# RWKV mixer: the first pair's preparation moved in among the feature projections

## The chip, the cores and the metric

The kernel runs on one core of one Trainium2 chip. A NeuronCore has a matrix engine (TensorE, PE), whose weight loads are shown apart as PEld, a vector engine (VectorE, DVE), an activation engine (ScalarE, ACT), GpSimd (POOL) and SyncE (SP), which here issues DMAs. The engines run their own instruction streams and wait for each other on semaphores. TensorE's clock is at 1.2 or 2.4 GHz; the profile gives it as the granted clock, 0.50 or 1.00. The metric is the device time of one execution in microseconds; smaller is better. The kernel before takes 3924.44 us (median of 3 runs, 3923.59 to 3925.01).

## The reference

One inference step of a two-layer decoder for 1024 prompt tokens and 8 x 8 sample tokens (1088 in all). Layer 0 has sparse attention (NSA) and RWKV-7 time mixing side by side, layer 1 gated linear attention (GLA); each is followed by a SwiGLU feed-forward. The change touches the RWKV-7 part only. Cut to what matters:

```
p  = rmsnorm(x) @ w_in                      # columns: r, k, v (512 each), xw 64, xa 64, xg 128
ps = p + mu * (p_prev - p)                  # token shift
z  = w0 + tanh(xw) @ wB;  w = exp(-exp(-softplus(-z) - 0.5))      # decay
a  = sigmoid(a0 + xa @ aB)
g  = sigmoid(xg) @ gB
kk = heads(k * k_k);  kk = kk * rsqrt(max(sum(kk * kk), 1e-24))
k  = heads(k * (1 + (a - 1) * k_a))
# per token and head: S = S*w + (S @ -kk)(kk*a)^T + v k^T;  y = S @ r
y  = groupnorm(y) * ln_w + ln_b + sum(r * k * r_k) * v           # the last term is the bonus
return y * g
```

## The kernel before

Activations lie transposed: 128 features on the partitions, 1088 tokens along the free axis, cut into chunks of 384, 384 and 320 (`CH`), so that one product of a 128-column weight tile is 8 x 3 matmuls into three PSUM banks. The 8 heads are worked as 4 pairs (128 columns). PSUM has 8 banks; the part at hand uses them as two groups of three, banks 0 to 2 and 3 to 5.

The program is a row of blocks. Each block is one function's instruction streams for all engines, and a barrier of all engines stands between two blocks. Around the change the row is: load inputs; `rmsnorm`; `rwkv_features`; `rwkv_prepare`; `rwkv_heads`; then `nsa_project` and the rest.

- `rwkv_features` projects five tiles in the order 0 to 4: tile 0 is xw and xa ("lora" below), tile 1 xg ("gate"), tiles 2, 3, 4 r, k, v of the first pair ("receptance", "keys", "values"). PE (L1422) fills one group of banks while ACT (L1435) copies the other to `raw`, and DVE (L1454, L1393 to L1397, L1457) mixes each token with the one before it. ACT then takes tanh (L1441) and sigmoid (L1443) of the two lora tiles. SP loads the weight tile after next as soon as a product is done (L1412).
- `rwkv_prepare` makes what the first pair's scan needs. PE: z (L1473), a (L1475), the sum of squares of kk over each head (L1480), the sum of the bonus (L1484). ACT: two sigmoids (L1491, L1494), a square root (L1497), three exponentials of the summed decay (L1499, L1501, L1503). DVE: everything between, with a reciprocal (L1527) and a scan (L1515), up to L1546.
- `rwkv_heads` scans the first pair while it projects and prepares the next ones; its first PE instruction is L1643 (scores of the first group of four 64-token chunks). The pieces beside its scan are set by a table written out by hand (`beside`), which the change does not touch.

The order on each engine is the order in which the code is written; no scheduler moves anything. A wait (`next`) is put on the engine's next instruction.

Of the kernel before, what the change touches and what calls it, by code (L numbers as in the profile page):

```python
# [17 lines left out]
ALU = mybir.AluOpType  # L18
# [4 lines left out]
P = 128  # L23
D = 1024
KT = D // P
NP = 1024
# [1313 lines left out]
def rwkv_mix(g, d, late):  # L1340
    nc = g.nc
    with ExitStack() as ctx:
# [29 lines left out]
        s = signals(nc, ctx, "rw_", "product raw_ready mixed_in za_ready kk_squared kk_summed kk_root "  # L1372
# [7 lines left out]
        rwkv_features(g, d, b, s, w_here, small)  # L1380
        rwkv_prepare(g, d, b, s, st_here)
# [18 lines left out]
def rwkv_features(g, d, b, s, w_here, small):  # L1400
    nc = g.nc
    tiles = range(5)
    with nc.Block() as block:
        @block.sync
        def _(sp):
            for i in range(2):
                sp.dma_start(b.w[i][:, :, :], d.w_rwkv[i]).then_inc(w_here[i], 16)
            sp.dma_start(b.lw[:, :, :].rearrange("p a n -> p (a n)"), d.lora).then_inc(small, 16)
            sp.dma_start(b.shift[:, :, :], d.shift).then_inc(small, 16)
            for i in tiles:  # L1410
                s.product.next(sp)
                sp.dma_start(b.w[i % 2][:, :, :], d.w_rwkv[RWKV_USES[i + 2]]).then_inc(w_here[i % 2], 16)  # L1412

        @block.tensor
        def _(pe):
            for x, i in enumerate(tiles):
                pe.wait_ge(w_here[i % 2], 16 * (i // 2 + 1))
                if x >= 2:
                    s.raw_ready.next(pe)
                for k in range(KT):  # L1420
                    for c, (o, n) in enumerate(CH):
                        mm = pe.matmul(g.ps[:, 3 * (x % 2) + c, 0:n], b.w[i % 2][:, k, :], g.act[:, k, o:o + n], start=(k == 0), stop=(k == KT - 1))  # L1422
                s.product.mark(mm)
            s.raw_ready.next(pe, 2)

        @block.scalar
        def _(act):
            seen = 0
            for x, i in enumerate(tiles):
                s.product.next(act)  # L1430
                if x >= 2 and seen < x - 1:
                    s.mixed_in.next(act, x - 1 - seen)
                    seen = x - 1
                for c, (o, n) in enumerate(CH):
                    a = act.activation(b.raw[x % 2][:, o:o + n], g.ps[:, 3 * (x % 2) + c, 0:n], ACT.Copy)  # L1435
                s.raw_ready.mark(a)
                if i < 2:
                    s.mixed_in.next(act)
                    seen = x + 1
                    if i == 0:  # L1440
                        act.activation(b.lora[0:64, 0, :], b.lora[0:64, 0, :], ACT.Tanh)  # L1441
                    else:
                        act.activation(b.lora[:, 1, :], b.lora[:, 1, :], ACT.Sigmoid)  # L1443
            s.mixed_in.next(act, len(tiles) - seen)

        @block.vector
        def _(dve):
            for n, i in enumerate(tiles):
                out = b.lora[:, i, :] if i < 2 else (b.r[:, :], b.k[:, :], b.v[0])[i - 2]
                x = b.raw[n % 2]  # L1450
                s.raw_ready.next(dve)
                if i == 0:
                    dve.wait_ge(small, 32)
                dve.tensor_tensor(out[:, 1:NP], x[:, 0:NP - 1], x[:, 1:NP], ALU.subtract)  # L1454
                rwkv_mixed(dve, g, b, i, x, out)
                dve.drain()
                s.mixed_in.mark(dve.scalar_tensor_tensor(out, out, g.col["mu"][:, i:i + 1], x, ALU.mult, ALU.add))  # L1457


def rwkv_prepare(g, d, b, s, st_here):  # L1460
    nc = g.nc
    col = lambda name: g.col[name][:, 0:1]
    ps3 = lambda first: [(g.ps[:, first + c, 0:n], o, n) for c, (o, n) in enumerate(CH)]
    bonus_in = b.raw[1]
    with nc.Block() as block:
        @block.sync
        def _(sp):
            sp.dma_start(b.st8[:, :, :], d.srwkv[0]).then_inc(st_here, 16)

        @block.tensor  # L1470
        def _(pe):
            for p, o, n in ps3(0):
                pe.matmul(p, b.lw[0:64, 0, 0:P], b.lora[0:64, 0, o:o + n], start=True, stop=True)  # L1473
            for p, o, n in ps3(3):
                mm = pe.matmul(p, b.lw[64:P, 0, 0:P], b.lora[64:P, 0, o:o + n], start=True, stop=True)  # L1475
            s.za_ready.mark(mm)
            s.kk_squared.next(pe)
            s.a_ready.next(pe)
            for p, o, n in ps3(0):
                mm = pe.matmul(p, g.blk, b.e[:, o:o + n], start=True, stop=True)  # L1480
            s.kk_summed.mark(mm)
            s.bonus_in.next(pe)
            for p, o, n in ps3(3):
# [4 lines left out]
        def _(act):  # L1488
            s.za_ready.next(act)
# [3 lines left out]
            for p, o, n in ps3(3):  # L1493
                a = act.activation(b.a[:, o:o + n], p, ACT.Sigmoid, bias=col("a0"))  # L1494
            s.a_ready.mark(a)
            s.kk_root.next(act)
            s.sq_ready.mark(act.activation(b.e[:, :], b.e[:, :], ACT.Sqrt))  # L1497
            s.decay_read.next(act)
            s.decay.mark(act.activation(b.e[:, :], b.e[:, :], ACT.Exp))  # L1499
            s.decay_read.next(act)  # L1500
            s.decay.mark(act.activation(b.e[:, :], b.cum[:, :], ACT.Exp, scale=-1.0))  # L1501
            s.decay_read.next(act)
            s.decay.mark(act.activation(b.e[:, :], b.cum[:, :], ACT.Exp))  # L1503

# [1298 lines left out]
```

## Time and profile before

| what | value |
|---|---|
| median of 3 runs | 3924.44 us |
| profiled execution | 3919.16 us, span 3917.5 us |
| mean granted clock | 0.950 |
| PE, DVE, ACT, POOL busy | 90%, 37%, 21%, 14% |
| first matmul of `rwkv_features` | 53.27 us |
| first matmul of `rwkv_prepare` | 133.32 us |
| first matmul of `rwkv_heads` | 169.56 us |

Times within the span count from its start. A busy share is an average over stages that differ, so it does not tell what bounds the stage at hand; for that the timeline is read, where each row has the start, the duration, the engine, the line and, in brackets, how long the engine stood idle before and who released it. A product of fp32 operands shows as two records for each matmul.

### The profile page before, as it was taken

How to read it: one execution, taken by the hardware profiler on the slowest of the kernel's cores; microseconds unless marked ns; L12 is line 12 of the kernel's file. 1: busy time of each engine (PE TensorE's matmuls, PEld its weight loads, DVE VectorE, ACT ScalarE, POOL GpSimd, SP SyncE). 2: the span in 40 equal slices, each digit the busy share in tenths (PEclk: the TensorE clock that was granted, in tenths of full speed). 3: DMA queues.
4: the chain of work that ended last, by engine and by line, in shares of the span. 5: the costliest groups of instructions: out<-in, count | busy, mean ns of one | idle time of the engine just before them, and what ended most of it. 6: DMA issues, size and time to landing. Idle time of an engine off the chain costs nothing. (4 is left out here: it accounts for less than half of the span.)

```text
span 3917.5 us, 60103 instructions
## 1 busy us (share of the span) xinstructions
PE 3528.8 (90%) x24871; PEld 2937.1 (75%) x24871; DVE 1444.3 (37%) x2676; ACT 830.0 (21%) x1575; POOL 535.8 (14%) x362
## 2 busy tenths in 40 slices
PE   6698988798877857999999998999997999999996
PEld 3466666654545636999999997666656999999996
DVE  2445645532256654332222333223323332322331
ACT  1132221111045622211111111222212211111110
POOL 0000000001400002422222221000001422222221
PEclk9899999898879978999999999999998999999998
DMA  2000000012310022111111111211122111111112
GB/s 92 20 12 13 24 12 13 30 63 68 88 49 1 2 100 73 50 51 35 52 38 43 48 32 45 85 39 40 65 91 107 50 51 35 52 33 44 52 32 99
DMA packets 77161, 189.07 MB, mean 48 GB/s; under 512 B 30996, under 2 KB 45268, under 8 KB 73956
## 3 DMA queue, kind: packets, MB, share of 16 engines
q1 hardware_dynamic: 64164, 157.97, 12.1%
q0 software_dynamic: 8448, 27.27, 2.2%
q8 instruction: 142, 2.33, 0.2%
q10 hardware_dynamic: 4352, 1.05, 0.2%
q14 instruction: 55, 0.45, 0.0%
HBM read 161.34 MB, written 29.04 MB: 49 GB/s over the span
## 5 line engine op out<-in xcount | busy, mean ns | idle before, releaser
L224 PE MATMUL ps<-ff_x,ff_wh 128*128 128x384 f32 (+1 forms) x3960 | 774.9, 328 | 0.0
L224 PEld LDWEIGHTS ps<-ff_x,ff_wh 128*128 128x128 f32 x3960 | 668.7, 188 | 0.8
L224 PE MATMUL ps<-ff_x,ff_wl 128*128 128x384 f32 (+1 forms) x2112 | 465.5, 328 | 0.0
L224 PEld LDWEIGHTS ps<-ff_x,ff_wl 128*128 128x128 f32 x2112 | 360.8, 188 | 0.0
L531 DVE TENSOR_TENSOR resid<-resid,ps 128x384 f32 (+1 forms) x240 | 113.2, 527 | 383.7 <-PE ps L224 383.7
L2377 PE MATMUL ps<-act,gl_w 128*128 128x384 f32 (+1 forms) x768 | 243.5, 473 | 0.0
L224 PE MATMUL ps<-ff_hh,ff_dh 128*128 128x384 f32 (+1 forms) x1056 | 233.2, 328 | 4.6 <-DVE ff_hl L523 4.6
L224 PE MATMUL ps<-ff_hh,ff_dl 128*128 128x384 f32 (+1 forms) x1056 | 232.7, 328 | 0.0
L224 PE MATMUL ps<-ff_hl,ff_dh 128*128 128x384 f32 (+1 forms) x1056 | 232.7, 328 | 0.0
L2377 PEld LDWEIGHTS ps<-act,gl_w 128*128 128x128 f32 x768 | 144.2, 191 | 89.1 <-issue 9.3
L518 DVE TENSOR_TENSOR ff_prod<-ff_silu,ps 128x384 f32<-128x384 f32 x132 | 62.3, 527 | 349.6 <-PE ps L224 349.6
L224 PEld LDWEIGHTS ps<-ff_hh,ff_dh 128*128 128x128 f32 x1056 | 180.2, 188 | 5.8 <-DVE ff_hl L523 5.8
L224 PEld LDWEIGHTS ps<-ff_hl,ff_dh 128*128 128x128 f32 x1056 | 180.4, 188 | 0.0
L224 PEld LDWEIGHTS ps<-ff_hh,ff_dl 128*128 128x128 f32 x1056 | 180.3, 188 | 0.0
L290 POOL TENSOR_TENSOR ff_wl<-ff_w,ff_wh 128x1024 fp32r<-128x1024 f32 x44 | 111.9, 2542 | 500.3 <-ACT ff_wh L415 500.3
L1676 PE MATMUL ps<-rw_up,rw_low 64*64 64x128 f32 (+1 forms) x1632 | 135.0, 264 | 45.8 <-DVE rw_tri L2059 29.0
L511 DVE TENSOR_TENSOR ff_silu<-ff_stats,ps 128x384 f32<-128x384 f32 x132 | 62.3, 527 | 302.7 <-PE ps L224 302.2
L298 POOL TENSOR_TENSOR ff_dl<-ff_wd,ff_dh 128x512 fp32r<-128x512 f32 (+1 forms) x80 | 111.9, 1404 | 410.7 <-ACT ff_dh L423 410.7
L607 PE MATMUL ps<-np_w,act 128*128 128x512 f32 (+5 forms) x432 | 159.6, 529 | 1.5 <-DVE resid L682 0.9
L1749 PE MATMUL ps<-act,rw_w 128*128 128x384 f32 (+1 forms) x432 | 160.9, 505 | 0.0
L439 ACT ACTIVATE ff_silu<-ff_silu 128x1088 f32<-128x1088 f32 x44 | 49.1, 1115 | 512.7 <-DVE ff_silu L511 512.7
L423 ACT ACTIVATE ff_dh<-ff_wd 128x512 fp32r<-128x512 f32 (+1 forms) x80 | 53.0, 674 | 480.8 <-PE ps L224 426.0
(567 smaller groups left out, 5499.1 us busy)
## 6 DMA issues: line engine op xcount, KB each, us to landing
ff_w<-in_wg SPq DMA_DIRECT2D x44, 512.0 KB, 3.5
ff_w<-in_wu SPq DMA_DIRECT2D x44, 512.0 KB, 3.5
ff_wd<-in_wd POOLq DMA_DIRECT2D x48, 256.0 KB, 3.0
ff_wd<-in_wd POOLq DMA_DIRECT2D x32, 320.0 KB, 3.3
ns_past<-in_cache_slc SPq DMA_DIRECT2D x64, 128.0 KB, 2.1
rw_w<-in_w_rwkv SPq DMA_DIRECT2D x14, 512.0 KB, 3.6
np_w<-in_w_nsa SPq DMA_DIRECT2D x8, 652.0 KB, 8.1
resid<-in_x SPq DMA_DIRECT2D x1, 4352.0 KB
```

What stands on the lines that cost most here:

```text
L224: mm = pe.matmul(g.ps[:, bank + c, 0:n], w[:, k, :], x[:, o:o + n], start=(first and i == 0), stop=(last and i == 2))
L290: pool.tensor_tensor(wl[0][:, :, :], w[0][:, :, :], wh[0][:, :, :].bitcast(F32), ALU.subtract).then_inc(s.gate_lo, 1)
L298: pool.tensor_tensor(dl[t][:, 0:nf, :], wd[t][:, 0:nf, :], dh[t][:, 0:nf, :].bitcast(F32), ALU.subtract).then_inc(s.down_lo, 1)
L423: act.activation(dh[t][:, 0:nf, :], wd[t][:, 0:nf, :], ACT.Copy).then_inc(s.down_hi, 1)
L439: act.activation(silu[:, :], silu[:, :], ACT.Silu).then_inc(s.silu_done, 1)
L511: m = dve.tensor_tensor(silu[:, o:o + n], rs[:, o:o + n], g.ps[:, c, 0:n], ALU.mult)
L518: m = dve.tensor_tensor(prod[:, o:o + n], silu[:, o:o + n], g.ps[:, 3 + c, 0:n], ALU.mult)
L531: m = dve.tensor_tensor(r, r, g.ps[:, 3 * t + c, 0:n], ALU.add)
L607: mm = pe.matmul(g.ps[0:R, b + j, 0:n], x, w[:, k, o:o + n], start=(k == 0), stop=(k == KT - 1))
L1676: mm = pe.matmul(g.ps[h, 5, P * c + 64 * x0:P * c + 64 * x1], low, up, start=True, stop=True)
L1749: mm = pe.matmul(g.ps[:, bank(j, name), 0:m], b.w[n % 2][:, k, :], g.act[:, k, o:o + m], start=(k == 0), stop=(k == KT - 1))
L2377: mm = pe.matmul(out[:, 0:n], w[:, k, :], g.act[:, k, o:o + n], start=(k == 0), stop=(k == KT - 1))
```

## The change

`rwkv_prepare` is gone as a block. Its instructions stand inside `rwkv_features`, whose order of projections is now `RWKV_FIRST` = 0, 3, 2, 1, 4: lora, keys, receptance, gate, values. The two groups of three PSUM banks are used in turn by nine users: lora (banks 0 to 2), keys (3 to 5), receptance (0 to 2), length (3 to 5), z (0 to 2), a (3 to 5), gate (0 to 2), values (3 to 5), bonus (0 to 2). The temporaries that shared buffers with `raw` now use `bt[1]` and `kt[1]`, which the second pair needs only later. The state's load (`st8`) is issued behind the last weight load. Core of the diff:

```diff
-        rwkv_features(g, d, b, s, w_here, small)
-        rwkv_prepare(g, d, b, s, st_here)
+        rwkv_features(g, d, b, s, w_here, small, st_here)
...
+RWKV_FIRST = [0, 3, 2, 1, 4]
...
+    scratch, bonus_in = b.bt[1], b.kt[1]
...
+            project(LORA, 0)
+            project(KEYS, 1)
+            s.raw_ready.next(pe)
+            project(RECEPTANCE, 0)
+            s.raw_ready.next(pe)
+            s.kk_squared.next(pe)
+            for p, o, n in ps3(1):
+                mm = pe.matmul(p, g.blk, b.e[:, o:o + n], start=True, stop=True)
+            s.kk_summed.mark(mm)
+            s.raw_ready.next(pe)
+            pe.wait_ge(small, 32)
+            s.lora_ready.next(pe)
+            for p, o, n in ps3(0):
+                mm = pe.matmul(p, b.lw[0:64, 0, 0:P], b.lora[0:64, 0, o:o + n], start=True, stop=True)
+            s.z_ready.mark(mm)
+            s.kk_root.next(pe)
+            for p, o, n in ps3(1):
+                mm = pe.matmul(p, b.lw[64:P, 0, 0:P], b.lora[64:P, 0, o:o + n], start=True, stop=True)
+            s.za_ready.mark(mm)
+            s.log_ready.next(pe)
+            project(GATE, 0)
+            s.a_ready.next(pe)
+            project(VALUES, 1)
+            s.raw_ready.next(pe)
+            s.bonus_in.next(pe)
+            for p, o, n in ps3(0):
+                mm = pe.matmul(p, g.blk, bonus_in[:, o:o + n], start=True, stop=True)
+            s.bonus_sum.mark(mm)
```

On PE, before, the end of the last projection and the block behind it (L1422 projection, L1473 z, L1475 a, L1480 length, L1484 bonus; "waits" names the semaphores):

```order
93 L1422 MATMUL ps<-act,rw_w 128x320
94 L1403 UNCONDITIONAL_BRANCH [waits rw_raw_ready]
95 L1470 UNCONDITIONAL_BRANCH [waits barrier_Pool_Activation_PE_DVE_SP_release]
96 L1473 MATMUL ps<-rw_lora,rw_lw 128x384 x2
97 L1473 MATMUL ps<-rw_lora,rw_lw 128x320
98 L1475 MATMUL ps<-rw_lora,rw_lw 128x384 x2
99 L1475 MATMUL ps<-rw_lora,rw_lw 128x320
100 L1480 MATMUL ps<-rw_e,const 128x384 [waits rw_a_ready,rw_kk_squared]
103 L1484 MATMUL ps<-resid,const 128x384 [waits rw_bonus_in]
107 L1630 UNCONDITIONAL_BRANCH [waits barrier_Pool_Activation_PE_DVE_SP_release]
```

On PE, changed, the place between the third and the fourth projection, and the end (L1429 projection, L1439 length, L1445 z, L1449 a, L1458 bonus):

```order
59 L1429 MATMUL ps<-act,rw_w 128x320
60 L1439 MATMUL ps<-rw_e,const 128x384 [waits rw_kk_squared,rw_raw_ready]
63 L1445 MATMUL ps<-rw_lora,rw_lw 128x384 [waits rw_lora_ready,rw_small,rw_raw_ready]
66 L1449 MATMUL ps<-rw_lora,rw_lw 128x384 [waits rw_kk_root]
69 L1429 MATMUL ps<-act,rw_w 128x384 [waits rw_w_here1,rw_log_ready]
86 L1429 MATMUL ps<-act,rw_w 128x384 [waits rw_w_here0,rw_a_ready]
103 L1458 MATMUL ps<-resid,const 128x384 [waits rw_bonus_in,rw_raw_ready]
107 L1640 UNCONDITIONAL_BRANCH [waits barrier_Pool_Activation_PE_DVE_SP_release]
```

The nine matmuls of length, z and a moved from behind the fifth projection to behind the third, the length ahead of z and a, each group with a wait of its own; one barrier fell away.

On ACT, changed, the same place (L1468 copies a product, L1477 square root, L1480 and L1484 sigmoids of z and a, L1487, L1490 and L1492 exponentials, L1494 sigmoid of gate):

```order
21 L1477 ACT_TABLE_LOAD
22 L1477 ACTIVATE rw_e<-rw_e 128x1088 [waits rw_kk_root]
23 L1480 ACT_TABLE_LOAD
24 L1480 ACTIVATE rw_logw<-ps,param 128x384 [waits rw_z_ready]
27 L1484 ACTIVATE rw_a<-ps,param 128x384 [waits rw_za_ready]
30 L1487 ACT_TABLE_LOAD
31 L1487 ACTIVATE rw_e<-rw_e 128x1088 [waits rw_decay_read]
32 L1468 ACTIVATE resid<-ps 128x384 [waits rw_mixed_in,rw_product]
35 L1490 ACTIVATE rw_e<-rw_cum 128x1088 [waits rw_decay_read]
36 L1492 ACTIVATE rw_e<-rw_cum 128x1088 [waits rw_decay_read]
37 L1494 ACT_TABLE_LOAD
38 L1494 ACTIVATE rw_lora<-rw_lora 128x1088 [waits rw_mixed_in]
```

The square root, with its table, now stands ahead of the sigmoids, and the copy of the gate product between the first and the second exponential.

On DVE, changed, from the last product of the keys' length to the end of the block (L1523 maximum, L1526 reciprocal, L1541 to L1549 the scan's operands, L1507 the first operation of a mix, L1556 bonus):

```order
33 L1523 TENSOR_SCALAR rw_e<-ps 128x384 [waits rw_kk_summed]
36 L1526 RECIPROCAL rw_e<-rw_e 128x1088 [waits rw_sq_ready]
37 L1528 TENSOR_SCALAR rw_logw<-rw_logw 128x1088 [waits rw_log_ready]
41 L1535 TENSOR_SCALAR resid<-rw_a,param 128x1088 [waits rw_a_ready]
44 L1541 SCALAR_TENSOR_TENSOR rw_ar<-rw_kkn,rw_e 128x17x64 [waits rw_decay]
46 L1545 TENSOR_TENSOR rw_bt<-rw_kkn,rw_e 128x1088 [waits rw_decay]
48 L1507 TENSOR_TENSOR rw_lora<-resid 128x1023 [waits rw_raw_ready]
55 L1549 TENSOR_TENSOR rw_ar<-rw_r,rw_e 128x17x64 [waits rw_decay]
58 L1507 TENSOR_TENSOR rw_v<-rw_raw 128x1023 [waits rw_raw_ready]
65 L1556 TENSOR_TENSOR rw_bonus<-ps,rw_v 128x384 [waits rw_bonus_sum]
```

The mixes of gate and values moved behind the preparation's operations, and the bonus, which stood in the middle, is the last.

## Rows read from the trace of the kernel before

**Rows 1.** The page: busy time, and the loads of the RWKV weights (median us to landing last).

```profile
PE 3528.8 (90%) x24871; PEld 2937.1 (75%) x24871; DVE 1444.3 (37%) x2676; ACT 830.0 (21%) x1575; POOL 535.8 (14%) x362
...
rw_w<-in_w_rwkv SPq DMA_DIRECT2D x14, 512.0 KB, 3.6
```

**Rows 2.** Timeline, features: start us, us, engine line op, names, count, idle before.

```profile
53.27 56.95 PE L1422 MATMUL ps<-act,rw_w 128*128 128x384 f32 x180 [14.69 <-DMA rw_w<-in_w_rwkv]
...
70.04 1.20 ACT L1435 ACTIVATE rw_raw<-ps 128x384 f32<-128x384 f32 x3 [30.89 <-PE ps L1422]
...
99.29 1.20 ACT L1435 ACTIVATE rw_raw<-ps 128x384 f32<-128x384 f32 x3 [9.19 <-PE ps L1422]
...
113.92 1.20 ACT L1435 ACTIVATE resid<-ps 128x384 f32<-128x384 f32 x3 [13.43 <-PE ps L1422]
...
128.55 1.20 ACT L1435 ACTIVATE rw_raw<-ps 128x384 f32<-128x384 f32 x3 [13.43 <-PE ps L1422]
...
131.49 1.35 DVE L1457 SCALAR_TENSOR_TENSOR rw_v<-rw_v,param,rw_raw 128x1088 f32<-128x1088 f32 x1
```

**Rows 3.** Timeline, preparation up to the first matmul of the heads.

```profile
133.32 2.25 PE L1473 MATMUL ps<-rw_lora,rw_lw 64*128 64x384 f32 x3 [4.81 <-PEq L1403]
...
140.11 1.48 ACT L1494 ACTIVATE rw_a<-ps,param 128x384 f32<-128x384 f32 x3
...
141.74 3.97 PE L1480 MATMUL ps<-rw_e,const 128*128 128x384 f32 x6 [3.02 <-ACT rw_a L1494]
142.27 2.42 DVE L1515 TENSOR_TENSOR_SCAN rw_cum<-const,rw_logw 128x1088 f32<-128x1088 f32 x1
...
145.74 1.42 DVE L1518 TENSOR_SCALAR rw_e<-ps 128x384 f32<-128x384 f32 x3 [1.05 <-PE ps L1480]
...
147.20 1.11 ACT L1497 ACTIVATE rw_e<-rw_e 128x1088 f32<-128x1088 f32 x1 [4.30 <-DVE rw_e L1518]
...
150.59 6.95 DVE L1527 RECIPROCAL rw_e<-rw_e 128x1088 f32<-128x1088 f32 x1
...
160.18 1.41 DVE L1534 TENSOR_TENSOR rw_bonus<-ps,rw_v 128x384 f32<-128x384 f32 x3
...
169.15 0.11 DVE L1546 MEMSET rw_st<- 128x64 f32 x1
...
169.56 0.69 PE L1643 MATMUL ps<-rw_ar,rw_bt 64*64 64x128 f32 x4 [14.85 <-PEq L1465]
```

**Rows 4.** Windows: us, busy PE, PEld, DVE, ACT, POOL, granted clock, DMA.

```profile
56.00:57.00 1.00, 1.00 (x3) 0.67 (x2) 0.00 (x0) 0.00 (x0) 0.00 (x0) 0.50 0.00 0
57.00:58.00 1.00, 1.00 (x4) 0.57 (x3) 0.00 (x0) 0.00 (x0) 0.00 (x0) 0.99 0.00 0
...
133.00:134.00 1.00, 0.68 (x1) 0.50 (x2) 0.68 (x1) 0.00 (x0) 0.00 (x0) 0.50 0.00 0
...
145.00:150.00 5.00, 0.71 (x2) 0.00 (x0) 4.09 (x6) 2.39 (x2) 0.00 (x0) 0.84 0.00 0
...
172.00:173.00 1.00, 1.00 (x14) 1.00 (x12) 0.00 (x0) 0.00 (x0) 0.00 (x0) 0.50 0.00 0
...
133.00:169.20 36.20, 13.37 (x24) 6.68 (x24) 27.03 (x24) 9.84 (x12) 0.00 (x0) 0.55 0.02 7
```

**Rows 5.** Timeline, heads: two short PE gaps; a table load and what follows.

```profile
177.24 0.34 PE L1676 MATMUL ps<-rw_up,rw_low 64*64 64x64 f32 x4 [2.34 <-DVE rw_tri L2059]
...
233.16 0.34 PE L1676 MATMUL ps<-rw_up,rw_low 64*64 64x64 f32 x4 [1.97 <-DVE rw_tri L2059]
...
234.79 1.28 ACT L1952 ACT_TABLE_LOAD   x1
236.09 1.11 ACT L1952 ACTIVATE rw_logw<-rw_logw 128x1088 f32<-128x1088 f32 x1
```

**Rows 6.** Windows, in the first gap and behind the second, columns as in rows 4.

```profile
175.00:176.00 1.00, 0.00 (x0) 0.00 (x0) 0.93 (x3) 0.98 (x3) 0.00 (x0) 1.00 0.00 0
...
236.00:237.00 1.00, 1.00 (x4) 0.55 (x2) 0.00 (x0) 0.99 (x2) 0.00 (x0) 0.50 0.00 0
```

More of the change, by code:

```diff
@@ L1414, in _ @@
[L1414 to L1457, printed above, removed]
@@ L1460, in rwkv_prepare @@
[L1460 to L1467, printed above, removed]
+                sp.dma_start(b.w[x % 2][:, :, :], d.w_rwkv[RWKV_FIRST[x + 2] if x < 3 else RWKV_USES[x + 2]]).then_inc(w_here[x % 2], 16)
             sp.dma_start(b.st8[:, :, :], d.srwkv[0]).then_inc(st_here, 16)
@@ L1488, in _, with raw @@
         def _(act):
-            s.za_ready.next(act)
+            def raw(x, half):
+                s.product.next(act)
+                if x >= 2:
+                    act.wait_ge(s.mixed_in.sem, x - 1)
+                for p, o, n in ps3(half):
+                    a = act.activation(b.raw[x % 2][:, o:o + n], p, ACT.Copy)
+                s.raw_ready.mark(a)
+            raw(LORA, 0)
+            act.wait_ge(s.mixed_in.sem, LORA + 1)
+            s.lora_ready.mark(act.activation(b.lora[0:64, 0, :], b.lora[0:64, 0, :], ACT.Tanh))
+            raw(KEYS, 1)
+            raw(RECEPTANCE, 0)
+            s.kk_root.next(act)
+            s.sq_ready.mark(act.activation(b.e[:, :], b.e[:, :], ACT.Sqrt))
+            s.z_ready.next(act)
             for p, o, n in ps3(0):
@@ L1492, in _ @@
             s.log_ready.mark(a)
-            for p, o, n in ps3(3):
+            s.za_ready.next(act)
+            for p, o, n in ps3(1):
                 a = act.activation(b.a[:, o:o + n], p, ACT.Sigmoid, bias=col("a0"))
             s.a_ready.mark(a)
-            s.kk_root.next(act)
-            s.sq_ready.mark(act.activation(b.e[:, :], b.e[:, :], ACT.Sqrt))
             s.decay_read.next(act)
             s.decay.mark(act.activation(b.e[:, :], b.e[:, :], ACT.Exp))
+            raw(GATE, 0)
             s.decay_read.next(act)
@@ L1503, in _ @@
             s.decay.mark(act.activation(b.e[:, :], b.cum[:, :], ACT.Exp))
+            act.wait_ge(s.mixed_in.sem, GATE + 1)
+            act.activation(b.lora[:, 1, :], b.lora[:, 1, :], ACT.Sigmoid)
+            raw(VALUES, 1)
         @block.vector
@@ L1508, in _, with mixed @@
             chunked = lambda x: x.rearrange("p (c t) -> p c t", t=64)
+            def mixed(x):
+                i = RWKV_FIRST[x]
+                out = b.lora[:, i, :] if i < 2 else (b.r[:, :], b.k[:, :], b.v[0])[i - 2]
+                y = b.raw[x % 2]
+                s.raw_ready.next(dve)
+                dve.tensor_tensor(out[:, 1:NP], y[:, 0:NP - 1], y[:, 1:NP], ALU.subtract)
+                rwkv_mixed(dve, g, b, i, y, out)
+                dve.drain()
+                s.mixed_in.mark(dve.scalar_tensor_tensor(out, out, g.col["mu"][:, i:i + 1], y, ALU.mult, ALU.add))
@@ L1509, in _ @@
+            dve.memset(b.st[0][:, :], 0.0)
+            dve.wait_ge(small, 32)
+            mixed(LORA)
+            mixed(KEYS)
+            dve.drain()
             dve.tensor_scalar(b.kk[:, :], b.k[:, :], col("kk"), None, ALU.mult)
             dve.drain()
+            s.kk_squared.mark(dve.tensor_tensor(b.e[:, :], b.kk[:, :], b.kk[:, :], ALU.mult))
+            mixed(RECEPTANCE)
+            s.kk_summed.next(dve)
+            for p, o, n in ps3(1):
+                m = dve.tensor_scalar(b.e[:, o:o + n], p, 1e-24, None, ALU.max)
@@ L1517, in _ @@
[L1517 to L1523 removed]
+            dve.drain()
+            s.decay_read.mark(dve.tensor_tensor(b.e[:, :], b.cum[:, :], b.lw_[:, :], ALU.subtract))
+            s.a_ready.next(dve)
@@ L1530, in _ @@
-            dve.drain()
-            s.decay_read.mark(dve.tensor_tensor(b.e[:, :], b.cum[:, :], b.lw_[:, :], ALU.subtract))
-            s.bonus_sum.next(dve)
-            for p, o, n in ps3(3):
-                dve.tensor_tensor(b.bonus[0][:, o:o + n], p, b.v[0][:, o:o + n], ALU.mult)
             s.decay.next(dve)
```

53 lines of the change are left out of this document (27 added, 26 removed).

## The prediction

> **What bounds the kernel now.** First the page as a whole [rows 1]: TensorE (PE) is busy 90% of the 3917.5 us span, VectorE (DVE) 37%, ScalarE (ACT) 21%. The stages are fenced off from one another by barriers, so the change acts in one place, between the first weight load of the RWKV mixer and the first matmul of `rwkv_heads`. The timeline of the features stage comes next [rows 2]: PE starts at 53.27 and streams without a gap; the five products reach ACT at 70.04, then 14.63 us apart, the third at 99.29, the fifth at 128.55; so 14.63 us for each projection, 0.61 us for each of its 24 matmuls. PE is the bound there: ACT (1.20 us) and DVE (until 131.49 + 1.35 = 132.84) work 4.29 us behind each product, beside the next projection. The timeline of the preparation is the opposite [rows 3]: from 133.32 to 169.26 DVE sets the end and PE is mostly idle. Its chain is z and a matmuls, sigmoids, the length of k, square root, a reciprocal of 6.95 us, three exponentials; only at 169.56 does PE start on the first group. So from the last product (128.55) to the first head matmul (169.56) 41.0 us pass in which PE has twelve matmuls.
>
> The granted clock is the last view [rows 4]: 0.50 until 57 us, when the projections have run for 3.7 us, 0.99 from there, 0.50 again at 133, and still 0.50 at 172. These are the 1.2 and 2.4 GHz levels. The first 3.7 us of projecting ran at half, which cost 1.87 us; a projection that starts at full clock thus needs 70.04 - 53.27 - 1.87 = 14.90 us from its first matmul to ACT's copy.
>
> **The change, part by part.** PE's order becomes lora, keys, receptance, then nine small matmuls (squared length, z, a), then gate, values, then three bonus matmuls. The number of matmuls is the same (120 + 12), as are the seven weight loads and the DVE operations; one barrier goes.
>
> *What goes:* the stretch from the product at 128.55 to 169.56, 41.0 us.
>
> *What is put between receptance and gate.* Receptance's stream ends where the fourth of before starts, 113.92 - 14.90 = 99.02. The length matmuls need 3 x 0.61 = 1.83 us (to 100.9), z another 1.83 (to 102.7; ACT's copy, which they wait for, is done at 99.29 + 1.20). Then PE waits for `kk_root`: DVE mixes receptance until 99.29 + 4.29 = 103.58 and takes the maximum, 1.42 us, until 105.0. PE does the a matmuls from 105.1 to 107.0 and waits again, now for z's sigmoid, which frees the banks: square root 1.11 us after 105.04, table load 1.28, sigmoid 1.48 as for a, which gives 108.94, and 0.15 us on the way to PE (as from the a sigmoid's end at 141.59 to L1480 at 141.74 [rows 3]). Gate starts at 109.09: 10.07 us put on PE's path, of which 4.5 are idle, in two gaps of 2.4 and 2.1 us.
>
> The change has five table loads in this region instead of four, and one of them lies on this path. The load's price is from a row: 1.28 us, and the next activation starts 0.02 us later [rows 5]. The other loads lie in ACT's idle time, and the one in front of the first z sigmoid of the heads goes. The Trainium skill (ScalarE: Activation LUTs, What ACT_TABLE_LOAD costs) adds a drain of about 1.38 us behind every load and advises against switching sets; by that the gate projection would start 1.4 us later and the time be 1.4 us higher. The trace does not show that drain.
>
> *What stands behind.* Gate's product reaches ACT at 109.09 + 14.90 = 123.99, values' 14.63 later at 138.62. Then copy and mix 4.29 us (142.91), a drain I put at 0.05 and the bonus products 1.41 [rows 3] (144.37). The bonus matmuls (1.83 us) run beside the mix. To the first head matmul there lie 0.30 us before (169.26 to 169.56), 0.48 at the other barrier (132.84 to 133.32); with 0.4 the heads start at 144.77. Saving without any clock effect: 169.56 - 144.77 = 24.8 us.
>
> *Is DVE in time for values?* Its preparation was 27.0 us of work [rows 4], the reciprocal (6.95) and the scan (2.42) the longest pieces [rows 3]. Of that kk and its square (some 2 us) now lie behind keys, and the bonus (1.41) comes last: 23.6 us remain, and the mix of gate, 4.29 less the copy, 3.1. From 103.58 on these 26.7 us, 1.2 of waiting for the square root, some 1.3 of waiting for the second exponential, which is queued on ACT behind gate's copy (123.99 + 1.20 + 1.11 = 126.3), and 0.6 for drains end at 133.4. Values are there for DVE at 138.62 + 1.20 = 139.8, so 6.4 us of slack cover all of it; each microsecond beyond would be lost one for one. What is queued behind the waits on PE is only the next projection, and the last exponential and gate's sigmoid end near 133, before ACT is wanted at 138.62. The weights of gate and values are loaded after the second and third products (84.7, 99.3), are there 3.6 us later [rows 1] and have over 20 us. SP's load of the state is issued behind the fifth product as before; its user is the last of the first pair's five groups.
>
> *The clock, which the trace of before shows only by neighbours.* In the new gaps PE does 1.83 us of work between two idle times of over 2 us. Nearest rows: after an idle time of 1.97 us before 233.16 the clock stood at 0.50 at 236, and in a longer one, 2.34 us before 177.24, it held 1.00 [rows 5, 6]. So both happen. If it falls, the a matmuls take up to 3.7 us, which the sigmoid of z covers (both end near 108.9), and gate loses half of the time that it runs low: with 0 and 3.7 us (what the first projection needed) the bounds are 0 and 1.9 us, or 3.7 with a second fall right behind. I take 1.6: the gaps are two, and in before the z and a matmuls (from 133.32) did not bring the clock back: L1480 behind them still took 3.97 us, not 1.83, and only then it rose (0.84 on average from 145 to 150) [rows 3, 4]. At the heads' start the clock is low in before, from 169.56 to about 173 [rows 4]. After, PE idles from 140.4 to 144.77, and in before 4.8 us without matmuls ended at 0.50 [rows 3, 4]: I count no difference; the bounds are 1.7 us gained (it is not low at all) and 1.7 lost (low twice as long).
>
> The Trainium skill (TensorE: Matmul & The Clock Gate, A second HAM failure mode: psum-queue depth-cycling) says that a kernel which cycles through PSUM banks and lets PE idle briefly between groups of matmuls makes the clock go back and forth between its levels. That rule speaks for the fall and against the 24.8; the trace agrees in the gap before 233.16 and not in the one before 177.24.
>
> **Sum.** -41.0 (stretch that goes) + 10.07 (put between) + 6.15 (138.62 to 144.77) = -24.8; +1.6 for the clock: -23.2. On the profiled execution: 3919.16 - 23.2 = 3896.0 (span 3894.3; 1.66 us lie around the span). The median of before is 5.28 above its profiled execution, so 3924.44 - 23.2 = 3901.2. All stages behind are fenced by barriers and start earlier by as much.
>
> **Rivals.**
> 1. The clock holds through both gaps. For it the gap before 177.24, against it the one before 233.16. Saves 24.8: 3899.6.
> 2. The gaps cost more: two low spells behind each other, or a longer one at the heads' start. 24.8 - 3.7 - 1.7 in the worst case; typically saves 20: 3904.4.
> 3. DVE becomes the bound. With gate half a spell later and waits across three engines the slack of 6.4 us would have to be used up, against it the sum above. With 9 us of lateness 2.6 us are lost: 3903.8.
> 4. Slower than before: the clock falls in the gaps and stays low through gate and values. Place: the two projections behind the gaps; price: their 29.26 us once more, 3924.44 - 24.8 + 29.26 = 3928.9. It decides once 24.8 of those 29.26 us of work run at 1.2 GHz. Against it: steady projecting brought the clock to 0.99 within 3.7 us [rows 2, 4]. By the rule of the Trainium skill named above (TensorE: Matmul & The Clock Gate) it would swing back and forth, which costs about half of that.
> 5. The reordering does not shorten the critical path, because PE waits in the new places for what it waited for in the old: 3924. Against it: DVE is busy 27.0 of the 36.2 us of preparation [rows 4], and all of it but the bonus rests on lora, keys and receptance, which now come first.
>
> **How the numbers follow.** Forecast 0.55; rival 1 0.24; rival 2 0.12; rival 3 0.05; rival 4 0.02; rival 5 0.02. Measurement and the chance position of low spells in the heads stage behind (one like that in [rows 6], if 3.4 us long as the one at 169.56, costs 1.7 us) add about 2 us to either side. The forecast with rival 1 reaches down to 3897.5; upward, with rivals 2 and 3, to 3905. Faster by over 0.2% (7.8 us, about what a measurement of this kernel tells from no change): 0.97, within 0.2% 0.01, slower 0.02.
>
> **What would show it.** In the profile after: products at ACT 70.0, 84.7, 99.3, then 124 to 126 and 138.6 to 140.5; two PE gaps of 2.4 and 2.1 us before gate; first head matmul at 144.7 to 146.5; DVE idle some 6 us before the values' mix; a clock of 0.50 somewhere between 104 and 113. Wrong would be: PE idle in front of values, bonus products later than 5 us behind values' copy, or a heads stage that is longer than before by more than 3 us.

## The result: faster, by more than forecast

In the first comparison the changed kernel takes 3891.22 us (median of 6 runs, 3884.77 to 3906.39), the kernel before 3924.02 (6 runs, 3910.27 to 3925.41); ratio 0.993 [0.9904, 0.9955]. The forecast was 3901.2, its range 3897.5 to 3905.0: the median is 6.3 us below the range. The sign was right, the time was not.

The profiled execution of the changed kernel tells another story than the medians. It took 3902.3 us (span 3900.6) where that of before took 3919.16: 16.9 us less, not 32.8. It is one of the six runs and the second slowest of them. The means of the two sixes differ by less than the medians: 3921.1 and 3893.5, 27.6 us. The page, of which this is the line of busy time (engine, us, share of the span, instructions):

```profile
PE 3534.5 (91%) x24871; PEld 2940.7 (75%) x24871; DVE 1444.1 (37%) x2676; ACT 829.1 (21%) x1575; POOL 536.1 (14%) x362
```

does not differ from [rows 1] in anything that explains it. The span has to be cut at the change. These are the windows of the kernel after, from the first projection to the first matmul of the heads, from there to the last matmul of the heads stage, and the rest (us from and to; length; busy time of PE, PEld, DVE, ACT, POOL with counts; granted clock, DMA share, GB/s):

```profile
53.08:146.16 93.08, 86.87 (x264) 52.37 (x265) 41.71 (x58) 21.90 (x32) 0.00 (x0) 0.94 0.12 40
146.16:757.28 611.12, 525.58 (x7566) 399.39 (x7566) 309.41 (x708) 159.75 (x343) 11.90 (x3) 0.94 0.04 13
757.28:3900.50 3143.22, 2904.12 (x16994) 2478.46 (x16993) 1073.34 (x1882) 635.60 (x1192) 523.76 (x354) 0.95 0.16 54
```

and the same stretches of the kernel before:

```profile
53.27:169.56 116.29, 88.60 (x264) 53.16 (x265) 42.02 (x59) 20.63 (x31) 0.00 (x0) 0.84 0.10 33
169.56:774.02 604.46, 518.61 (x7566) 394.70 (x7566) 309.18 (x708) 161.32 (x344) 11.91 (x3) 0.95 0.04 13
774.02:3917.40 3143.38, 2904.13 (x16993) 2478.93 (x16993) 1073.59 (x1882) 636.10 (x1192) 523.44 (x354) 0.95 0.17 54
```

The stretch that was changed is 23.21 us shorter (116.29 to 93.08), against 23.2 forecast. PE's work in it is the same. Everything behind the heads is equal within 0.2 us. But the heads stage, whose code is unchanged, took 6.66 us longer, with 7 us more PE busy time for the same 7566 matmuls: they ran slower. -0.19 (start) - 23.21 + 6.66 - 0.16 = -16.9.

The stretch itself, in rows picked from the timeline of the kernel after (start, duration, engine, line, operation, out<-in; in brackets the idle time before and its releaser):

```profile
99.41 1.20 ACT L1468 ACTIVATE rw_raw<-ps 128x384 f32<-128x384 f32 x3 [13.43 <-PE ps L1429]
101.13 2.09 PE L1445 MATMUL ps<-rw_lora,rw_lw 64*128 64x384 f32 x6
105.06 1.11 ACT L1477 ACTIVATE rw_e<-rw_e 128x1088 f32<-128x1088 f32 x1 [3.15 <-DVE rw_e L1523]
105.08 3.89 PE L1449 MATMUL ps<-rw_lora,rw_lw 64*128 64x384 f32 x6 [1.86 <-DVE rw_e L1523]
106.19 1.28 ACT L1480 ACT_TABLE_LOAD   x1
107.48 1.47 ACT L1480 ACTIVATE rw_logw<-ps,param 128x384 f32<-128x384 f32 x3
109.01 31.02 PE L1429 MATMUL ps<-act,rw_w 128*128 128x384 f32 x96
125.43 1.20 ACT L1468 ACTIVATE resid<-ps 128x384 f32<-128x384 f32 x3 [5.48 <-PE ps L1429]
140.06 1.20 ACT L1468 ACTIVATE rw_raw<-ps 128x384 f32<-128x384 f32 x3 [5.72 <-PE ps L1429]
141.29 1.23 DVE L1507 TENSOR_TENSOR rw_v<-rw_raw 128x1023 f32<-128x1023 f32 x1 [6.74 <-ACT rw_raw L1468]
144.44 1.42 DVE L1556 TENSOR_TENSOR rw_bonus<-ps,rw_v 128x384 f32<-128x384 f32 x3
146.16 0.69 PE L1653 MATMUL ps<-rw_ar,rw_bt 64*64 64x128 f32 x4 [4.31 <-PEq L1411]
```

Read it as the chain of PE: receptance's product at 99.41, z at 101.13, then an idle time until DVE's maximum (L1523) ends, the a matmuls at 105.08, gate from 109.01 on, released by z's sigmoid (L1480). Gate's product comes 16.42 us after its first matmul, values' 14.63 later, the heads 6.10 behind that. All three stand within 0.1 us of the forecast's terms (14.90 + 1.6, 14.63, 6.15).

And the clock of the same execution in single windows between 104 and 113 us:

```profile
104.00:105.00 1.00, 0.00 (x0) 0.00 (x0) 1.00 (x3) 0.00 (x0) 0.00 (x0) 1.00 0.00 0
105.20:106.00 0.80, 0.80 (x2) 0.49 (x3) 0.00 (x0) 0.80 (x1) 0.00 (x0) 0.52 0.00 0
106.00:109.00 3.00, 2.97 (x5) 1.10 (x4) 2.80 (x1) 2.92 (x5) 0.00 (x0) 0.50 0.00 0
109.00:112.00 3.00, 2.99 (x5) 1.78 (x6) 3.00 (x1) 2.75 (x4) 0.00 (x0) 0.50 0.02 5
112.00:113.00 1.00, 1.00 (x4) 0.64 (x4) 1.00 (x1) 0.00 (x0) 0.00 (x0) 0.97 0.00 0
```

PE comes into the gap at 1.00, is at 0.50 (1.2 GHz) from about 105.2, does the a matmuls in 3.89 us and the first 3.0 us of gate at half, and is back just after 112.0. Half of those 3.0 us is the 1.5 us by which gate's product (16.42) exceeds the 14.90 of a projection at full clock.

So two questions are left for the experiments: is the saving 23 us with the rest due to something else, or is it really larger; and what makes the heads stage 7 us longer in one execution.

### The profile page after: what moved, and what is told of

Its sections match the earlier page's. It is cut to its first block and busy times, and to the rows that moved or that the text cites. A ratio compares the mean times of both kernels' runs of the same rounds, so it can differ in the third digit from the quotient of the medians.

```text
span 3900.6 us, 60095 instructions
## 1 busy us (share of the span) xinstructions
PE 3534.5 (91%) x24871; PEld 2940.7 (75%) x24871; DVE 1444.1 (37%) x2676; ACT 829.1 (21%) x1575; POOL 536.1 (14%) x362
```

## The experiments

The theory under test: the terms of the forecast hold one by one, the saving is about 23 us, and the rest of the 32.8 lies in the level at which each series happened to run. Its main rival: the changed kernel saves about 30 us, and the time comes from somewhere that the forecast did not count. The two times of the first comparison cannot tell these apart; more runs and more profiles of the same two kernels can.

### The two kernels again

No edit in either.

> The changed kernel once more. Theory A (the path became 23.2 us shorter as forecast, and what the runs show beyond it is the chance position of the spells of low clock, above all in the heads stage): features to heads again 93 us in the profile (92 to 95), the stages from the NSA projection on equal to before within 1 us each, the heads stage anywhere from 595 to 612 us, with half of the difference in low time between any two profiles as their difference in length; runs spread again over 10 to 20 us, and the mean saving over all runs is 20 to 29 us. Theory B (the change makes the heads stage itself shorter by some 10 us in most runs): the mean saving stays at 30 to 35 us, and the heads stage of this profile is below 600 us.

> The kernel before once more. Theory A: its own runs spread too (3910 to 3925 so far), its heads stage in the profile differs from 604.5 us by half of the difference in low time, features to heads is 116.3 us within 1. Theory B: its heads stage stays at 604 within 1 us, and its runs stay at 3924 but for single ones.

Measured: after 3893.58 us (5 runs, 3891.61 to 3897.91), before 3917.95 (15 runs), ratio 0.9941 [0.9927, 0.9954]; the copy of before 3918.68 (11 runs), ratio 1.0008 [0.9999, 1.0017]. The runs of that copy lie between 3915.93 and 3923.23, but for one of 3934.12. The changed kernel stayed at its level, the kernel before came out 6 us lower than in the first comparison. The windows of this profile of the kernel after:

```profile
51.93:143.96 92.03, 85.84 (x265) 51.99 (x265) 41.73 (x58) 21.93 (x32) 0.00 (x0) 0.95 0.13 41
143.96:748.03 604.07, 518.47 (x7566) 394.25 (x7566) 309.67 (x708) 160.12 (x343) 11.91 (x3) 0.96 0.04 13
453.80:465.80 12.00, 11.27 (x212) 9.03 (x212) 7.92 (x22) 6.55 (x14) 0.00 (x0) 1.00 0.24 88
```

The stretch again measures 92.0, but the heads are at 604.07, as in before. The third window stands some 310 us into the heads. The same place in the first profile of the kernel after:

```profile
456.00:468.00 12.00, 11.74 (x113) 8.83 (x114) 4.41 (x13) 3.27 (x7) 0.00 (x0) 0.57 0.14 53
```

Clock 0.57 against 1.00, 113 matmuls against 212 in the same 12 us: a low spell of 10.2 us that one execution has and the other doesn't. The heads stage spent 68.3 us at the low clock in the first and 54.3 in the second; half of the difference is 7.0, and the stages differ by 7.05. The second profile of the kernel before (stretch 116.12, heads 604.38) has the same low time in the heads as the first within 0.3 us, so it does not separate the theories; it does show that the stage comes out the same when the low time does. So the longer heads stage is not a cost of the change.

### The clock held through the gaps

```
         z's three matmuls
+        keep_busy((384, 384, 384, 192))    # matmuls into bank 6, which nobody reads
         a's three matmuls
+        keep_busy((384, 384, 384))
...
         the bonus sum's three matmuls
+        keep_busy((384,) * 6)
```

> The changed kernel with 13 more matmuls into an unused PSUM bank: four behind z, three behind a, six behind the bonus sums, so that TensorE has hardly any idle time there. Theory A: the clock stays at 1.00 through gate and values and at the start of the heads; gate's product reaches ACT at 124.0 instead of 125.4, features to heads 91.7 us instead of 93.1, and the first group of the heads 1.7 us shorter: 2.5 to 3.5 us less than the changed kernel up to there; over whole runs hidden by the spread. Rival (the gate projection is not slowed by the clock but by what ACT and DVE do beside it): gate's product stays at 125.4.

Measured: 3896.3 us (3889.35 to 3898.06, 5 runs), ratio 0.9943 [0.9929, 0.9956]; the stretch is 92.07. In its timeline, and in a window over gate and values:

```profile
109.63 29.42 PE L1429 MATMUL ps<-act,rw_w 128*128 128x384 f32 x96
124.46 1.20 ACT L1475 ACTIVATE resid<-ps 128x384 f32<-128x384 f32 x3 [4.54 <-PE ps L1429]
```

```profile
109.63:138.90 29.27, 29.27 (x98) 18.25 (x97) 21.50 (x22) 8.74 (x11) 0.00 (x0) 1.00 0.06 18
```

Gate starts 0.6 us later (the last filler stands in its way) and its product comes 14.83 us after, not 16.42: the clock in the gaps costs 1.6 us, the value taken in the sum, and the rival (gate slowed by what ACT and DVE do beside it) is out. Of this the filler returns 1.0 us against the first profile (93.08 to 92.07; Theory A had 91.7), which whole runs, with their spread, don't show. The stretch itself varies by more than that without any edit (92.03 to 94.33, below).

### The gate projection ahead of the a matmuls

```
             s.kk_root.next(pe)
-            for p, o, n in ps3(1):          # the a matmuls
+            project(GATE, 1)
+            s.log_ready.next(pe)
+            for p, o, n in ps3(0):          # the a matmuls
...
-            s.log_ready.next(pe)
-            project(GATE, 0)
+            s.raw_ready.next(pe)
+            project(VALUES, 1)
             s.a_ready.next(pe)
-            project(VALUES, 1)
-            s.raw_ready.next(pe)
```

ACT does the first exponential and gate's copy ahead of a's sigmoid, and DVE the first product with it earlier; ACT has one table load more.

> The changed kernel with the gate projection moved ahead of the a matmuls (gate in banks 3 to 5 as soon as the maximum has read them, a behind it in banks 0 to 2), so that TensorE does not wait for z's sigmoid; on ACT a's sigmoid moves behind gate's copy, with one more table load. Theory A (TensorE's order sets the end, DVE has 6 us of slack): the gap of 2 us goes, values' product comes at 136.4 to 138 instead of 140.1, features to heads 89.5 to 91.5 us. Rival (DVE's chain has no room for a later a): the values' mix starts late and features to heads stays at 93 us or grows.

Measured: 3901.1 us (3895.68 to 3908.27, 5 runs), ratio 0.9952 [0.9938, 0.9966]: 7 us slower in the mean than the kernel after on the same chip (3900.8 against 3894.0), though the stretch is shorter, as Theory A had it (values' product at 138.14, 0.1 above its 138). Its profile is that of its slowest run. Its windows: the stretch, the heads, and 18 us of the heads from 8 us behind their start.

```profile
52.92:144.25 91.33, 85.14 (x265) 51.60 (x265) 41.90 (x58) 24.62 (x34) 0.00 (x0) 0.95 0.13 41
144.25:763.54 619.29, 533.68 (x7566) 406.38 (x7566) 309.70 (x708) 160.30 (x343) 11.91 (x3) 0.93 0.04 13
152.00:170.00 18.00, 13.55 (x162) 12.64 (x162) 3.89 (x11) 3.21 (x9) 0.00 (x0) 0.53 0.01 1
```

The heads are 15.2 us longer than in the second profile of the kernel after (604.07), at 35.8 us more of low clock. The 0.7 to 1.8 us gained in front of the stage are worth less than where its low spells fall. Whether the 17 us spell comes with this edit or by chance, one profile cannot show.

### The order of projections alone

In the kernel before, with `rwkv_prepare` still a block of its own:

```
+RWKV_FIRST = [0, 3, 2, 1, 4]
-            for x, i in enumerate(tiles):
+            for x, i in enumerate(RWKV_FIRST):
...
-            for n, i in enumerate(tiles):
+            for n, i in enumerate(RWKV_FIRST):
```

SP's weight loads and ACT's waits for the mixes follow the same order.

> The kernel before with the new order of projections alone (lora, keys, receptance, gate, values), the preparation still a block of its own behind a barrier. Theory A: the order by itself moves nothing; features to heads 116 us within 1, time that of before within the spread. Rival (the order itself brings part of it, by what DVE and ACT find ready): features to heads 113 us or less.

Measured: 3921.36 us (10 runs, 3913.35 to 3924.16) against 3919.07 (17 runs) for before, ratio 1.0004 [0.9995, 1.0013]. The stretch is 117.49, 0.5 us outside Theory A's 116 within 1 and on the side away from the rival; the clock was low for the first 6.28 us of projecting here and for 3.83 us in the kernel before, and half of the difference is 1.2 us. In the heads, 8 us behind their start, there is a 17 us spell like that of the experiment before:

```profile
52.02:58.30 6.28, 6.28 (x10) 3.53 (x11) 0.00 (x0) 0.00 (x0) 0.00 (x0) 0.50 0.32 127
52.02:169.51 117.49, 89.46 (x265) 53.73 (x265) 42.01 (x59) 20.63 (x31) 0.00 (x0) 0.83 0.10 32
177.00:195.00 18.00, 13.51 (x160) 12.60 (x160) 3.98 (x12) 3.44 (x10) 0.00 (x0) 0.53 0.00 1
```

The order by itself gives nothing; the gain comes only when the preparation no longer stands behind the products. How much of it the preparation would bring with the old order of projections, no run shows.

### DVE's slack used up

```
+            dve.reciprocal(b.y[0], g.act[:, 0, :])
+            dve.drain()
+            dve.reciprocal(b.y[0], g.act[:, 0, :])
             mixed(VALUES)
```

> The changed kernel with two reciprocals of 6.95 us (into a tile that nobody reads) on DVE ahead of the mix of values, 13.9 us of work where the profile after has 6.7 us of idle time. Theory A (DVE has that slack and becomes the bound beyond it): features to heads 93 + 13.9 - 6.7 = 100.3 us, 99.5 to 101.5. If the slack is not real (something else already holds the end): 93 + 13.9 = 107. If DVE's chain has nothing to do with the end: 93.

Measured: 3908.37 us (3904.15 to 3909.92, 6 runs), ratio 0.997 [0.9958, 0.9982]. In the timeline:

```profile
134.38 6.94 DVE L1552 RECIPROCAL rw_y<-act 128x1088 f32<-128x1088 f32 x1
139.97 1.20 ACT L1468 ACTIVATE rw_raw<-ps 128x384 f32<-128x384 f32 x3 [5.73 <-PE ps L1429]
141.40 6.95 DVE L1554 RECIPROCAL rw_y<-act 128x1088 f32<-128x1088 f32 x1
148.27 1.16 DVE L1507 TENSOR_TENSOR rw_v<-rw_raw 128x1023 f32<-128x1023 f32 x1
153.07 0.69 PE L1656 MATMUL ps<-rw_ar,rw_bt 64*64 64x128 f32 x4 [11.31 <-PEq L1411]
```

This execution has the slack and the loss in it. DVE was free for the mix of values at 134.4, and the values were copied at 139.97 + 1.20 = 141.2: 6.8 us of slack. The two reciprocals take 13.9 us, and the mix starts at 148.27, 7.1 us after the values were there. The stretch is 101.33, 7.0 us longer than in the profile of the kernel after on the same chip (94.33, next section). So DVE was off PE's path by about the 6.4 us of the sum, and what goes past it is lost one for one: DVE is next in line, the mechanism of rival 3.

### The kernel after, third and fourth series

No edit. These are the companions of the experiments around them, and give the level and the spread.

> The changed kernel a third time. Theory A (path 23 to 25 us shorter, the rest chance position of low clock): mean saving over the runs 20 to 29 us, median 3890 to 3900; profile features to heads 92 to 94 us, heads stage 604 us if its low time is 54 us, plus half of any low time above. Theory B (33 us is the true saving, the second series was the unlucky one): median saving 30 us or more.

> The changed kernel a fourth time. Theory A (the saving is 23 to 25 us, the rest is where the low spells of the clock fall): mean saving 20 to 29 us over this series, and over all series together 22 to 27 us. Theory B (33 us): 30 or more.

Measured: 3897.94 us (3893.3 to 3905.99, 5 runs) against 3919.07 (17 runs), ratio 0.9948 [0.9934, 0.9961]; and 3893.64 (3892.81 to 3902.18, 5 runs) against 3918.19 (9 runs), ratio 0.9947 [0.9934, 0.9961]. The heads took 608.12 and 604.19 us, with 64.9 and 54.4 us at the low clock. The mean savings, 20.9 and 22.1 us, lie where Theory A put them, and Theory B's 30 did not come. The stretch took 94.33 and 92.45. In the four profiles it is longer where more of it ran at the low clock: 10.1, 10.5, 11.2 and 12.9 us of low clock for 92.03, 92.45, 93.08 and 94.33. In the third series' profile the long spell stands near the start of the heads and not 310 us in:

```profile
153.30:163.50 10.20, 7.75 (x96) 7.22 (x96) 2.12 (x6) 2.31 (x7) 0.00 (x0) 0.50 0.00 0
456.00:468.00 12.00, 11.27 (x178) 8.52 (x176) 7.80 (x19) 5.31 (x10) 0.00 (x0) 1.00 0.34 94
```

Its 10.5 us more of low clock than in the second profile cost 4.05 us (608.12 - 604.07), less than half. PE was busy for 7.75 of the 10.2 us, and half of that is 3.9.

### The pieces beside the scan ahead of the inverse

The rest is about the heads. PE waits there for the triangular step of DVE (`rw_tri`), 29.0 us in 17 waits. This edit gives PE the first piece of each group ahead of the inverse that waits, not behind it.

```
+                        if c == 0:
+                            beside(j, 8 * i)
                         inverse(j, i + 1, 2 * c)
-                        beside(j, 8 * i + 2 * c)
+                        if c:
+                            beside(j, 8 * i + 2 * c)
```

> The changed kernel, and in the heads stage the first piece of projection of each group (beside, every eighth) put ahead of the first inverse step instead of behind it, so that TensorE has work while DVE masks the scores. Theory A (the idle time of about 2 us at 16 of the group starts, 29 us in all before, and the low spells that follow it are lost time): heads stage 575 to 592 us instead of 604, low time there 20 to 45 us instead of 54, whole time 3865 to 3885. Rival (the inverse is a chain of round trips between TensorE, DVE and ACT, and starting it later only moves the wait): heads stage 600 us or more.

Measured: 3884.15 us (3882.94 to 3895.85, 5 runs), ratio 0.9918 [0.9904, 0.9931]; 12 us in the mean below the kernel after of the same chip (3886.2 against 3898.35, with a standard error of 3.4). The waits in the heads (who <- for whom: us in total, times, longest), in the kernel after:

```profile
PE ps L1686 <- DVE rw_tri L2069: 29.0, 17, 2.3
```

and here, with the window of the heads:

```profile
PE ps L1686 <- DVE rw_tri L2072: 8.7, 7, 2.3
PE ps L1767 <- DVE rw_e L2185: 7.3, 3, 2.4
```

```profile
145.37:739.30 593.93, 520.58 (x7566) 394.76 (x7566) 309.72 (x708) 159.28 (x343) 11.91 (x3) 0.95 0.04 14
```

20.3 us of one wait go and 7.3 of a new one come, 13.0 in all. The stage agrees, if its low time (61.3 us, against 54.3 in the second profile of the kernel after) is counted at half: 604.07 - 593.93 + 3.5 = 13.6. Theory A was right on the whole time and on the cause, not on the size: it had a stage of 575 to 592 us and a low time of 20 to 45 us. The waits went, but the low time did not fall, so by this profile the gain is the idle time alone. The rival's stage of 600 us or more did not come.

### The start of the heads filled

```
             the bonus sum's three matmuls
+            for n in (384,) * 6:
+                pe.matmul(g.ps[:, 6, 0:n], g.blk, g.act[:, 0, 0:n], ...)
...
             scores(0, 0)
+            for n in (384,) * 3:
+                pe.matmul(g.ps[:, 7, 0:n], g.blk, g.act[:, 0, 0:n], ...)
```

> The changed kernel with six matmuls into an unused bank behind the bonus sums and three more behind the first scores of the heads, where TensorE waits for DVE's masks. Theory C (the part of the spread that comes from the heads' start: a clock that falls at the first masks stays low for 10 to 17 us, since the inverse steps behind them leave TensorE idle half of the time): no low spell in the first 25 us of the heads, heads stage 600 to 605 us in the profile, runs within 8 us of each other and 2 to 6 us faster in the mean than the changed kernel. Rival (the spells are decided later in the stage): no difference in mean and spread.

Measured: 3896.06 us (3892.7 to 3902.68, 5 runs), ratio 0.9944 [0.993, 0.9957]. Windows of the first 25 us of the heads, of the place 310 us into them, and of the whole stage:

```profile
146.47:171.50 25.03, 19.11 (x338) 16.60 (x338) 7.25 (x19) 5.46 (x15) 0.00 (x0) 1.00 0.01 2
456.50:468.50 12.00, 11.94 (x115) 9.03 (x116) 4.21 (x12) 3.08 (x7) 0.00 (x0) 0.57 0.12 45
146.47:757.57 611.10, 527.48 (x7572) 399.64 (x7572) 309.56 (x708) 159.99 (x343) 11.91 (x3) 0.94 0.04 13
```

The low spell at the start is gone, the one at 456.5 is there, and the stage took 611.10 us where Theory C had 600 to 605. Neither the time nor the spread improved (mean 3897.6 against 3896.7 on the same chip). So the heads' start alone does not decide between shorter and longer executions. The long spell fell 310 us in here and in the first profile of the kernel after, and 7 us in in that of the third series.

### Both, and all three

The two edits above together, and then with the gate projection ahead of the a matmuls as well; no further edit.

> The last one together with the projection pieces ahead of the first inverse step (as in the run before that had them alone: 12 us faster than the changed kernel). Theory C: 14 to 18 us faster than the changed kernel in the mean, heads stage 585 to 594 us. Rival: 12 us, as without the filling.

> The same with the gate projection ahead of the a matmuls as well. Its part up to the heads was 1.8 us shorter than in the changed kernel's first profile and 0.7 us shorter than in its second, but its heads began with a low spell of 17 us. Theory C (that spell was what made that kernel slower, and the filling takes it away): features to heads 91 to 92 us, heads stage as in the run without it, whole time 1 to 2 us below that one. Rival (gate ahead of a costs elsewhere): above it.

Measured: both 3884.8 us (3880.12 to 3887.65, 5 runs), ratio 0.9911 [0.9897, 0.9924]; all three 3880.09 (3877.03 to 3887.1, 4 runs), ratio 0.99 [0.9885, 0.9915]. The last is the fastest kernel of this case and beats both given ones: mean 3881.1, 15.6 us below the kernel after of the same chip (3896.7). Both alone are 12.5 us below it (mean 3884.2), with the heads at 597.49 us: the rival's 12, not the 14 to 18 us and 585 to 594 us of Theory C. The windows of all three, of the stretch and of the heads:

```profile
52.60:143.40 90.80, 88.48 (x277) 53.59 (x277) 41.89 (x58) 24.59 (x34) 0.00 (x0) 0.96 0.13 41
143.40:742.05 598.65, 527.19 (x7572) 399.24 (x7572) 309.91 (x708) 159.35 (x343) 11.91 (x3) 0.94 0.04 14
```

With the start of the heads filled, gate ahead of a takes the stretch from 93.13 to 90.80 us and the mean from 3884.2 to 3881.1, without a low spell in the first 90 us of the heads. With 4 and 5 runs, this 3 us is a pointer, not a proof.

## Why the prediction was wrong, step by step

**The change itself was right.** Point by point, forecast and first profile: receptance's product 99.3 and 99.41; PE idle 1.86 us ahead of the a matmuls for 2.4 (the length and z matmuls end at 103.22, forecast 102.7), while the second gap is gone, filled by the a matmuls at half the clock, as the clock term had it; gate starts 109.09 and 109.01; its product 124 to 126 and 125.43; values' 138.6 to 140.5 and 140.06; DVE idle before the values' mix 6.4 and 6.74 (both its ends lie over 1 us later than in the sum, 134.56 for 133.4 and 141.26 for 139.8, so the slack comes out better than its parts); first head matmul 144.7 to 146.5 and 146.16; clock 0.50 somewhere between 104 and 113, and there it is. The saving of the stretch is 23.21 us for 23.2, and in the other three profiles of the kernel after the stretch is 92.03, 94.33 and 92.45 (before: 116.29 and 116.12), so 23.2 is not luck in one execution. It is not exact to a tenth either: the four have a mean of 93.0.

**The clock term** (+1.6) was right in size: 16.42 - 14.90 = 1.5 here, 1.6 by the filled gaps. The prediction had bounds of 0 and 1.9, neighbouring rows that pointed both ways, and counted on two gaps where there was one; that it hit within 0.1 is partly luck. The clock fell in all four profiles of the kernel after, so rival 1 (it holds) did not happen, nor did it stay low as rival 4 needed: 0.97 at 112. The rule of the Trainium skill weighed in the prediction (TensorE: Matmul & The Clock Gate, A second HAM failure mode: psum-queue depth-cycling) pointed to the fall, and the trace agrees with that half of it; the swing back and forth through gate and values, the other half, did not come.

**The table load** on PE's path cost its own 1.28 us: loaded at 106.19, the next activation starts at 107.48. The further drain of about 1.38 us that the Trainium skill (ScalarE: Activation LUTs, What ACT_TABLE_LOAD costs) puts behind each load is not seen.

**Rivals 2, 3 and 5** did not happen: the heads start where forecast, DVE has its slack (and is next, by the doubled reciprocal), and PE's waits did become shorter. The low clock in the gaps lasted 6.8 us in each of the four profiles, with no second spell right behind it. Rival 2's longer spell at the heads' start does stand in one of them, that of the third series (10.2 us from 153.3).

**What failed is the last two steps, those that turn a saving into a time.** One is the base: "The median of before is 5.28 above its profiled execution, so 3924.44 - 23.2 = 3901.2". Three runs within 1.4 us of each other looked like a level. Over all series, 58 runs of the kernel before have a mean of 3919.2 (median 3918.15, standard deviation 3.4): 5 us lower, and by chance where its profiled execution stood. From there 3919.2 - 23.2 = 3896.0, the number that the prediction itself worked out for the profiled execution and then raised. In the first comparison itself the kernel before did stand at 3924.02, but the kernel after did not stand 5 us high with it, so that level was not one that both share. The 21 runs of the kernel after have a mean of 3895.5 (median 3893.64, standard deviation 6.0). The difference of the means is 23.65 us with a standard error of 1.4, so 20.9 to 26.4, if the runs are taken as independent; by series it is 27.6, 23.9, 20.9 and 22.1. The difference of the medians of all runs is 24.5. The forecast saving lies among them, and the 32.8 of the first medians outside.

The other is the allowance, "the chance position of low spells in the heads stage ... about 2 us to either side". It was priced by a single spell of 3.4 us, "as the one at 169.56". That one was misread: what reaches into the heads there is the end of a spell of 23.9 us in the kernel before.

```profile
149.20:173.10 23.90, 7.53 (x46) 5.40 (x48) 18.58 (x16) 3.73 (x4) 0.00 (x0) 0.50 0.00 1
```

The runs of the kernel after spread over 21.6 us, and the spells that make the difference between its profiles are longer: 10.2 us at one of two places in the kernel after, 17 us in two experiments. In the first six runs the order of the times is the order of the granted clocks: 3884.77 at 0.957, 3885.28 at 0.956, 3888.04 at 0.955, 3894.40 at 0.953, 3902.30 at 0.952, 3906.39 at 0.949. As an estimate, 0.008 of clock over 3890 us is 62 us more at half speed, for 21.6 us of time. With a standard deviation of 6.0 a median of six has a standard error of 1.25 x 6.0 / sqrt(6) = 3.1 us, so 3.9 us to either side 8 times in 10, before any term of the sum is in doubt. Around 3896.0 that is 3892 to 3900; the 3891.2 of the first comparison lies just outside it, at 1.5 standard errors. One of the prediction's own signs of error, a heads stage longer by more than 3 us, was met (6.66) and pointed to just this.

**Open.** Why four of the first six runs of the kernel before stood at 3923.6 to 3925.4 and why three of the first six of the kernel after stood at 3885 to 3888, lower than any of its 15 later ones, was not settled: there is a profile only of one run in each series, and none of such a run. The latter three had granted clocks of 0.955 to 0.957, the other 18 runs 0.949 to 0.955, so they had less low time, but where, no trace shows. Nor is it shown what starts the long spell in the heads, or what puts it near their start or 310 us in; filling the start did not remove the later one.

## What to carry to other kernels

Price a moved block by PE's chain alone: where the next projection can start, what each wait in the new place waits for, and how far behind DVE stands; here this gave 23.2 us for a measured 23.65 (standard error 1.4). Do not put such a saving on a level from three runs that happen to agree: take the spread of many runs of the kernel before, and widen the range where the stages behind are made of short waits in which the clock can fall. Where PE waits again and again for about 2 us, useful work put ahead of the wait (12 us) was worth more here than filler that only holds the clock (no change to be seen in whole runs).

## What the runs showed of the hardware

- Low spells of the granted clock in a stage of short waits cost at most about half their length. In the heads, 14.0 us more at 0.50 cost 7.05 us, 10.5 us more 4.05 (third series) and 35.8 us more 15.2 (gate ahead of a). As an estimate, the cost is half of PE's busy time in the spell: PE was busy for 11.74 of the 12 us around the first and for 7.75 of 10.2 in the second.
- The same code had 54.3 to 68.3 us of low clock in the heads from one execution of the kernel after to the next.
- One idle time of 1.86 us between small matmuls was followed by 6.8 us of low clock (105.2 to 112.0); with the idle time filled the clock stayed at 1.00.
- A 17 us spell (clock 0.53 from 152 to 170) appeared 8 us into the heads where the stage started at 144.25, and none where it started at 143.96; one with the heads at 169.51, and none of that length inside the heads that start at 169.56. The start time alone does not set it.
- Not all low time costs: later runs of the kernel before at a mean clock of 0.953 and at 0.949 both took 3918 us.
